# Samples' cached keys: turned by VectorE in 32x32 blocks instead of by TensorE, gathered in column blocks of 32 channels

## The reference

```
for l in range(2):
    h = rms_norm(x) * (1 + scale) + shift
    zq, zk, zv, zqi, zki, zwi, zga, zglu, zgc, zmerge = split(h @ w_in[l])     # 2048 x 10832 weights
    q, k, qi, ki = rope(...)                       # 8 query heads, 2 key heads of 128; indexer of 16 heads of 64
    # samples: keys and values of the past come through the page table
    k_all = concat([cache_k[l][page_table], k]);  v_all = ...;  ki_all = concat([cache_kidx[l][page_table], ki])
    score = sum_h relu(qi . ki_all) * wi;  keep the top 256 keys of each query
    attn = softmax(q . k_all[kept] / sqrt(128)) @ v_all[kept]
    y_att = (attn * silu(zga)) @ w_attn_out
    y_conv = conv branch (GLU, 31 taps, layer norm, silu) @ w_conv_out
    x = x + gate * ((g_att * y_att + g_conv * y_conv) @ w_out)
```

## Time and profile before

| | us |
|---|---|
| median of 3 runs | 3471.35 (3469.75 to 3474.79) |
| the profiled execution, device time | 3470.14 |
| its span on the page | 3468.4 |
| PE busy | 3388.4 (98%) |
| PEld busy | 3164.7 (91%) |
| DVE busy | 1812.6 (52%) |
| POOL busy | 1232.9 (36%) |
| ACT busy | 1045.9 (30%) |
| mean share of the 16 DMA engines in use by the SP queue | 56.2% |

### The profile page before, as it was taken

How to read it: one execution, slowest core, us unless ns; L and a number is a source line. 1 busy time by engine, 2 the same in 40 slices (tenths; PEclk the granted TensorE clock), 3 DMA queues, 4 the chain that set the end, 5 groups by cost and what they waited for, 6 DMA issues and landing times. The chain is left out here.

```text
span 3468.4 us, 66254 instructions
## 1 busy us (share of the span) xinstructions
PE 3388.4 (98%) x27454; PEld 3164.7 (91%) x27454; DVE 1812.6 (52%) x2535; ACT 1045.9 (30%) x1444; POOL 1232.9 (36%) x508
## 2 busy tenths in 40 slices
PE   6899999999999999999999999999999999999999
PEld 3699989889999989998888999898999998999998
DVE  1523468989986123332326244788889841233211
ACT  2322322223542333222213222322235423332211
POOL 0243333446324223333333433334362332233433
PEclk9899999999999999999999999999999999999999
DMA  9834444656545774658895656544332257744444
GB/s 327 281 106 118 111 109 124 186 174 199 157 132 162 232 241 161 207 194 292 289 297 172 185 166 187 141 124 111 103 115 77 84 187 233 228 138 137 129 131 96
DMA packets 591304, 593.09 MB, mean 171 GB/s; under 512 B 110876, under 2 KB 556337, under 8 KB 580923
## 3 DMA queue, kind: packets, MB, share of 16 engines
q1 hardware_dynamic: 588732, 588.59, 56.2%
q10 hardware_dynamic: 2272, 0.28, 0.1%
HBM read 546.37 MB, written 116.39 MB: 191 GB/s over the span
## 5 line engine op out<-in xcount | busy, mean ns | idle before, releaser
L869 POOL TENSOR_TENSOR w_lo_t<-raw,w_hi_t 128x1024 fp32r<-128x1024 f32 x472 | 1187.7, 2517 | 2211.4 <-ACT w_hi_t L882 2211.4
L1180 PE MATMUL acc<-act_hi,w_hi_t 128*128 128x272 f32 x6528 | 1392.2, 294 | 20.4 <-POOL w_lo_t L869 11.8
L1180 PE MATMUL acc<-act_hi,w_lo_t 128*128 128x272 f32 x6528 | 1353.9, 289 | 0.0
L1180 PE MATMUL acc<-act_lo,w_hi_t 128*128 128x272 f32 x6528 | 1349.7, 288 | 0.0
L1180 PEld LDWEIGHTS acc<-act_hi,w_hi_t 128*128 128x128 f32 x6528 | 1028.7, 189 | 90.7 <-issue 68.8
L1180 PEld LDWEIGHTS acc<-act_lo,w_hi_t 128*128 128x128 f32 x6528 | 1029.0, 189 | 0.0
L1180 PEld LDWEIGHTS acc<-act_hi,w_lo_t 128*128 128x128 f32 x6528 | 1022.9, 189 | 0.0
L882 ACT ACTIVATE w_hi_t<-raw 128x1024 fp32r<-128x1024 f32 x472 | 499.9, 1059 | 1642.6 <-PE acc L1180 1629.9
L1755 DVE SCALAR_TENSOR_TENSOR conv<-conv,cw 128x512 f32<-128x512 f32 x240 | 241.2, 1005 | 29.6 <-POOL w_lo_t L869 29.6
L1180 PE MATMUL acc<-m_hi,w_hi_t 128*128 128x272 f32 x1024 | 215.2, 292 | 0.0
L1180 PE MATMUL acc<-m_lo,w_hi_t 128*128 128x272 f32 x1024 | 211.5, 288 | 0.0
(11 more groups left out here) (244 smaller groups left out, 2586.3 us busy)
## 6 DMA issues: line engine op xcount, KB each, us to landing
raw<-in_w_in_dram SPq DMA_DIRECT2D x272, 512.0 KB, 3.8
ada_ring<-in_w_ada_dram SPq DMA_DIRECT2D x95, 512.0 KB, 7.2
raw<-in_w_in_dram SPq DMA_DIRECT2D x136, 256.0 KB, 3.3
k_near<-in_cache_k_dram SPq DMA_DIRECT2D x256, 128.0 KB, 2.7
v_near<-in_cache_v_dram SPq DMA_DIRECT2D x256, 128.0 KB, 2.7
k_ring<-k_near SPq DMA_DIRECT2D x64, 512.0 KB, 5.1
v_page<-v_near SPq DMA_DIRECT2D x64, 512.0 KB, 6.5
raw<-in_w_out_dram SPq DMA_DIRECT2D x64, 512.0 KB, 4.1
```

The costliest lines, as they stand in the source:

```text
L869: pool.tensor_tensor(w_lo_t[:, m % 2], raw[:, m % 4], w_hi_t[:, m % 2].bitcast(F32), ALU.subtract).then_inc(S.w_lo, 1)
L1180: last = pe.matmul(acc[:, 2 * m + h, 0:HALF], w[:, c % 2, k, P * m:P * m + P], r[:, kt, h * HALF:(h + 1) * HALF], start=first and k == 0 a ...
```

## The change

1. The copy `k_near` has another layout: for each page the 2 heads and 4 blocks of 32 channels come first, then the 128 positions, then the 32 channels of the block. A page is still gathered by one DMA, which now reads and writes pieces of 32 numbers (128 bytes), 1024 of them, where before it moved 16 pieces of 8192 bytes.
2. The gather of keys stands apart from that of values, as the first work of the `aside`: one page per chunk in the groups 1 to 32, in both layers. In layer 0 it so comes on top of the indexer pages in the groups 1 to 16, with a page look-up of its own. The values keep their places in layer 0; in layer 1 they go one page per chunk in the groups 1 to 32 too.
3. `k_ring` is loaded so that a partition holds, for one block of 32 channels and one of 32 rows, runs of 128 numbers (512 bytes) for each page and head; DVE turns the 32x32 blocks of all 128x1024 numbers in one instruction, from `k_ring` straight to `k_t`, with the positions put back in order by the output's steps.
4. PE's 8 transposes, ACT's copy and DVE's copy are gone; `logits_s` waits for DVE's turn and reads `k_t` in four runs of 128 columns.

```diff
+def page_at(n, i):
+    return divmod(4 * (n - 1) + i, PAGES)
...
-        k_near = nc.dram_tensor("k_near", [DEPTH, SEQS, PAGES, PAGE, KVW], F32).ap()
+        k_near = nc.dram_tensor("k_near", [DEPTH, SEQS, PAGES, KVH, HD // BLK, PAGE, BLK], F32).ap()
...
-                sp.dma_start(k_ring[:, q % 3], k_near[l, b, 4 * j:4 * j + 4].rearrange("g p c -> p g c")).then_inc(k_landed[q % 3], 16)
+                src = k_near[l, b, 4 * j:4 * j + 4].rearrange("y g a (k m) i -> (a k) (y g) (m i)", m=PAGE // BLK)
+                sp.dma_start(k_ring[:, q % 3], src).then_inc(k_landed[q % 3], 16)
...
-            def gather(places, staged):
+            def gather(places, staged, keys=None):
...
+                    if keys is not None:
+                        near, cache = keys
+                        sp.dma_start(near[b, g].rearrange("h a k i -> (h a) k i"),
+                                     cache[ds(page, 1)].rearrange("y k (c i) -> (y c) k i", i=BLK)).then_inc(S.kv_staged, 16)
...
+                if l == 0 and 1 <= n < 33:
+                    gather([(page_at(n, i), [])], S.kv_staged, keys)
                 if l == 0 and 1 <= n < 17:
                     gather([(x, [(kx_near[a], cache_kidx[a]) for a in range(DEPTH)]) for x in staged_at(n, i)], S.kx_staged)
                 if l == 0 and 17 <= n < 33:
-                    gather([(x, kv) for x in staged_at(n - 16, i)], S.kv_staged)
-                if l > 0 and 1 <= n < 17:
-                    gather([(x, kv) for x in staged_at(n, i)], S.kv_staged)
+                    gather([(x, [values]) for x in staged_at(n - 16, i)], S.kv_staged)
+                if l > 0 and 1 <= n < 33:
+                    gather([(page_at(n, i), [values])], S.kv_staged, keys)
...
-                            act.activation(k_t[:, j, 0, :], aux[:, 0, :], ACT.Copy).then_inc(S.k_cp_a, 1)
...
-                        last = pe.transpose(aux[:, g, P * kk:P * kk + P], k_ring[:, q % 3, kk, g * HD:(g + 1) * HD], ident)
-                last.then_inc(S.k_turned, 1)
...
-                pe.wait_ge(S.k_cp_a, 32 * l + 4 * b + 4)
-                pe.wait_ge(S.k_cp_b, 32 * l + 4 * b + 4)
+                pe.wait_ge(S.k_turned, 32 * l + 4 * b + 4)
...
-                        pe.matmul(aux[32 * j:32 * j + 32, 2, :], q_blk[:, b, g, :], k_t[:, j, g, :], start=g == 0, stop=g == 1)
+                        pe.matmul(aux[32 * j:32 * j + 32, 2, :].rearrange("p (y n) -> p y n", n=PAGE), q_blk[:, b, g, :], k_t[:, j, g:4 * KVH:KVH, :], start=g == 0, stop=g == 1)
...
-            def keep_k(l, b, j):
-                dve.wait_ge(S.k_turned, 32 * l + 4 * b + j + 1)
+            def turn_k(l, b, j):
+                q = 32 * l + 4 * b + j
+                dve.wait_ge(k_landed[q % 3], 16 * (q // 3 + 1))
...
-                dve.tensor_copy(k_t[:, j, 1, :], aux[:, 1, :]).then_inc(S.k_cp_b, 1)
+                dve.transpose(k_t[:, j].rearrange("p x (k m) -> p x m k", m=PAGE // BLK),
+                              k_ring[:, q % 3].rearrange("p x (m i) -> p x m i", i=BLK)).then_inc(S.k_turned, 1)
```

More of the change, by code:

```diff
@@ L423, in trunk_kernel @@
         pt_p = at(C + 21408, "pt_p", [P, 2, 512])
-        k_ring = at(C + 16512, "k_ring", [P, 3, 4, KVW])
+        k_ring = at(C + 16512, "k_ring", [P, 3, 4 * KVH, PAGE])
         q_blk = at(C + 19584, "q_blk", [P, SEQS, KVH, NS])
@@ L435, in trunk_kernel @@
         z_t = at(C + 21176, "z_t", [SEQS, NS])
-        k_t = at(C + 11072, "k_t", [P, 4, KVH, 512])
+        k_t = at(C + 11072, "k_t", [P, 4, 4 * KVH, PAGE])
         bias_s = [at(C + 23456, "bias_s0", [P, 516]), at(C + 15176, "bias_s1", [P, 516])]
@@ L504, in trunk_kernel @@
             bias_done bias_stored logits_p praw_done exp_p rsum_done p_ready ptr_p ptc_p pv_p ao_p
-            k_landed0 k_landed1 k_landed2 k_turned k_cp_a k_cp_b logits_s brep_in0 brep_in1 sraw_done exp_s ps_ready pts_ps pts_done
+            k_landed0 k_landed1 k_landed2 k_turned logits_s brep_in0 brep_in1 sraw_done exp_s ps_ready pts_ps pts_done
             v_landed0 v_landed1 v_landed2 v_landed3 pv_s o_done peaks_ps peaks_done part_exp part_done part_ps w_done attn_ps ao_s
@@ L755, in aside @@
                     sp.dma_start(mask_t[:, :, :, :], table[:, T_MASK:N_TAB].rearrange("p (a b n) -> p a b n", a=2, b=SEQS)).then_inc(S.cs_in, 16)
-                kv = [(near[l], cache[l].rearrange("g p h d -> g p (h d)")) for near, cache in ((k_near, cache_k), (v_near, cache_v))]
+                keys, values = ((near[l], cache[l].rearrange("g p h d -> g p (h d)")) for near, cache in ((k_near, cache_k), (v_near, cache_v)))
+                if l == 0 and 1 <= n < 33:
+                    gather([(page_at(n, i), [])], S.kv_staged, keys)
                 if l == 0 and 1 <= n < 17:
@@ L1459, in window @@
                         turn_s(l, b)
-                    for j in range(4):
-                        if h == turn_at(b, j):
-                            turn_k(l, b, j)
                     if h == logits_at(b):
@@ L1966, in window @@
                         if h == turn_at(b, j):
-                            keep_k(l, b, j)
+                            turn_k(l, b, j)
                     if h == values_at(b):
```

## The result

The change made the kernel slower: 3492.15 us (median of 4 runs, 3490.14 to 3495.21) against 3471.09 us before; ratio 1.0056, 95% interval [1.0043, 1.0069]. The forecast was 3445 us, faster than before. The profiled execution of the changed kernel has a span of 3488.4 us, 20.0 us more than before.

The account below looks back on a forecast made before the run. PE, busy 98% of the span, was taken as the bound: 3470.1 - 57.0 (turn off PE) + 30.7 (PE waiting for SP) = 3443.8, with 1.2 for the median 3445 us; forecast's own range 3434 to 3468, full range 3412 to 3525.

Parts of the forecast that it names:

- part 3: Key gather on SP in groups 1 to 16 of layer 0: extra work there makes PE wait 30.7 us.
- the price of a page on SP: Each chunk in groups 1 to 16 of layer 0: look-up 0.76 plus DMA issue 0.79, 1.55 us.
- the tightest customer: Last tight tile behind SP's swaps: group 9's second query tile, 7.8 us to spare, 38 chunks with extra work before it.
- Part 1, PE: Samples' attention: 64 turns of 0.89 us leave PE, 57.0 us less; strided logits reads cost nothing.
- Part 2, DVE: Samples' attention: 64 DVE transposes of 1.42 us, at most 2.8, hidden; ring loads a microsecond or two longer, DMA share 0.84.
- The formula in between: From SP to PE: extra work 58.9, less SP's waits 20.4, less permitted lateness 7.8, leaves 30.7 us of PE waits.
- Groups 12 to 32: After the tight tile: 40.3 us of SP work against 35.5 of waits, 5 us more lateness, borne by weight loads.
- Rival A: SP held at the key DMA's issue, 1.84 us, so 2.60 us a page; slower, 3517 us in all; chance 0.34.
- Rivals B and C: B: PE does not notice SP, 3414 us, chance 0.12. C: slow pieces make PE wait for key data, chance 0.04.

Follow-up runs that it names:

- e1: Keys turned by DVE as in the changed kernel, but the gather of the kernel before: whole rows, old places; 3417.16 us, ratio 0.9847.
- e9: The changed kernel with another key DMA: 1024 pieces of 128 bytes, source read in order, outermost step 8, column blocks left out; 3490.76 us.
- e10: The changed kernel with a key DMA of 1024 pieces of 128 bytes, source read in order, outermost step 16, column blocks left out; 3461.37 us.
- e5: The changed kernel with the key DMA's steps reordered, 128 rows outermost instead of 8 column blocks, same pieces and places; 3460.18 us, ratio 0.9968.
- e12: The changed kernel with keys gathered in the places of the kernel before, in column blocks with 128 rows outermost; 3414.07 us, ratio 0.9834.
- e2: The changed kernel with keys gathered in the places of the kernel before, in column blocks with 8 blocks outermost; 3479.87 us, ratio 1.0019.
- e6: The changed kernel with unused matmuls added ahead of five PE waits, 36 at four and 88 at the fifth; 3491.99 us, ratio 1.0059.

## Why the prediction was wrong

The mechanism and its place were those of the forecast: SP's list in groups 1 to 16 of layer 0, through swap, rotation and eviction to PE. The gain was right. The loss was forecast at 30.7 us and was 79.6, and with that the sign turned. Of it 36.9 us fell in groups 3 to 6, where it was forecast, and 24.1 in group 11, where nothing was. Two steps of part 3 failed: the price of a page on SP (1.55 us, measured 2.17) and the choice of the tightest customer, that is of the instruction behind a swap that can bear the least lateness (group 9's second query tile with 7.8 us to spare; it was group 10's last, with 1.4). By the prediction's steps:

- **Part 1, PE: right.** 57.0 us forecast; 55.0 by e1's median, 56.0 in the change's own trace and in e1's. Reading four runs of 128 columns costs nothing: a logits matmul takes 592 ns in both kernels.
- **Part 2, DVE: right within its bound.** 2.01 us, not the 1.42 taken; the upper end was 2.8. No wait of PE for it. A ring load lands in 6.7 us against the 5.1 of the earlier trace rows, within the microsecond or two allowed; the DMA share of the stretch is 0.90 and not 0.84.
- **Part 3, the price per page: too low.** 0.76 + 0.79 = 1.55 us forecast, 2.17 measured. The two terms themselves were exact. Missing were the 0.5 us and more by which what stands behind the key DMA is held. The nearest row that I took, L694, has an outermost 8 and the same duration, but only 32 pieces, and nothing behind it is held; the trace of before, SP:

```profile
648.24 0.81 SPq L694 DMA_DIRECT2D out_dram<-u_tok  x1
649.09 2.08 SPq L623 DMA_DIRECT2D kx<-kx_near  x4
```

  Four loads in 2.08 us are 0.52 each. So the rows of before that I read did not show the hold, and an outermost 8 alone does not bring it. The range of 0.50 to 1.84 us that the prediction gives for the issue was wide enough to take it in; the value picked out of it was not.
- **Part 3, the tightest customer: wrong.** I took the second query tile of group 9, with 7.8 us to spare. The tightest is the last query tile of group 10, for which PE waits directly, in the transposes of the new keys. These rows of the kernel before (SP, DVE, then L1249 by line) were there to be read:

```profile
412.69 1.22 SPq L611 DMA_DIRECT2D stage<-stage  x2
```

```profile
420.95 0.72 DVE L1665 TENSOR_TENSOR q_att<-stage 128x544 f32<-128x544 f32 x1
```

```profile
L1249 PE MATMUL aux<-con,k_new x20: 270/272/273, 423.1 to 2134.5; 128*128 128x128 f32 x16, 128*32 128x128 f32 x4
```

  Rotation done at 421.7, PE there at 423.1: 1.4 us to spare, and 42 pages ahead of it, not 38. In the changed kernel:

```profile
485.10 1.22 SPq L616 DMA_DIRECT2D stage<-stage  x2
```

```profile
L1252 PE MATMUL aux<-con,k_new x20: 270/346/473, 494.1 to 2185.7; 128*128 128x128 f32 x16, 128*32 128x128 f32 x4
```

  The swap comes 72.4 us later, less 1.4 to spare, so PE comes 71.0 us later: 494.1 - 423.1.
- **The formula in between: not refuted, and only in part tested.** With the measured entries, 42 x 2.17 (extra time) - 19.8 (waits used up) - 1.4 + 1.2 (the first swap's own shift) = 71.1, against the 71.0 above. But 2.17 was taken from the swaps' own delay, so this tests the step from the swap to PE and not the price. The rows give the price by themselves: 0.76 + 0.79 + 0.49 (the longer look-up behind) = 2.04 us, times 41 pages 83.6 us; one indexer gather at 164 us that was held for 3.75 us in place of 0.50 adds 3.2. That is 86.8 of the 91.1 us; some 4 us no row accounts for. Of the difference between 30.7 and 74.7 us (up to group 12) the wrong customer makes 11.1 (42 x 1.55 - 21.9 - 1.4 = 41.8), the price 0.62 x 42 = 26.0, unused waits and the start 3.3, the low clock behind the last wait 3.7.
- **Groups 12 to 32: nearly right.** "5 us more lateness, which the weight loads can bear": they had more to bear, and PE lost 4.0 us in groups 18 to 21.
- **Rival A** (slower, 0.34) had the better part. It put the issue of the key DMA at 1.84 us, a quarter of the 7.37 of the earlier trace rows, so 2.60 us a page and 3517 us in all, which the upper end of the range, 3525, takes in. The time is between the forecast and that: the price was 2.17, beyond the 1.89 at which SP's delay on PE equals the 57 us that PE saves (64 x 1.89 - 20.4 - 7.8 - 35.5 = 57.3). That SP is held at its issue is half right: the key DMA's own row is 0.79 us, and the holding falls on the instruction behind it, 0.5 us of a look-up and 0.8 of a weight load. It hangs on the outermost step: 8 was dear (e9, 3490.76 us), 16 cheap (e10, 3461.37), 128 cheap (e5, 3460.18), and the semaphore records split in the same way, 9 updates with 8 outermost and 16 with the others. What holds SP no row here shows, neither few engines nor room in their queues. Nor is the full queue of the earlier trace rows shown as such: before, 1110 to 1117.4 us, the trace has four value loads in 7.37 us at a DMA share of 1.07, and a median of 0.45 us for one issue of that line in the whole span.
- **Rivals B and C: out.** PE did notice SP (against B), and there was no wait of PE for key data, as slow pieces (C) would have brought; with 128-byte pieces and all of SP's time given back (e12) the kernel is as fast as with whole rows (e1).

## What to carry to other kernels

Before an instruction is added to a full in-order queue, list every customer of what stands behind it with the time each has to spare (customer: what waits for it), also those that wait directly and not through an accumulator; the least spare time and the number of additions ahead of it set the price. Price a DMA on its issuing engine by the gap to the end of the next instruction, not by its own row. And write the steps of a DMA of many pieces so that the outermost one is not 8 but 16 or 128, the two that were tried, on both sides: in this kernel that was worth 32 us in the change's places and 66 us in the old ones (e2 against e12), for the same bytes to the same addresses.

## What the runs showed of the hardware

- A DMA of 1024 pieces with an outermost step of 8 took 0.76 to 0.78 us to issue and lengthened the next instruction on SP by 0.5 us (a register load, 0.74 us in place of 0.27) to 0.8 us (a weight load, 1.35 us in place of 0.58); with 16 or 128 outermost it took 0.57 us and held nothing. One of 32 pieces with an outermost 8 also took 0.79 us, but held nothing.
- With 8 outermost a DMA left 9 updates of its semaphore, with 16 or 128 outermost 16 (the change and e9 against e5 and e10).
- DVE's 32x32 transpose of 128x1024 in f32, with its output in steps, took 2.01 us, where 128x512 takes 0.71.
- PE's wait of 11.4 us in the change ended at 494.1 us, and the granted clock was 0.50 from 490 to 500:

```profile
490.00:500.00 10.00, 5.86 (x29) 5.12 (x30) 5.76 (x7) 1.28 (x1) 0.00 (x0) 0.50 0.44 97
```

  With PE's waits filled (e6) the stretch 430 to 560 us kept 0.99, and group 12 started only 2.7 us earlier: in this stretch, which SP paces, PE's clock was not what counted.
